# Attention and its output product of a two-layer decoder trunk: a fifth output slab is split ahead of the join, head statistics move behind a product step, and row scaling moves from VectorE to ScalarE

## The reference

```python
sc = jnp.einsum('bqhcd,bkhcd->bhcqk', qb, kb) * scale      # 8 heads, 2 components c of width 64
p = jax.nn.softmax(jnp.where(causal, sc, NEG_INF), axis=-1)
a = p[:, :, 0] - lam * p[:, :, 1]
outs.append(jnp.einsum('bhqk,bkhe->bqhe', a, vb))          # e = 128
...
o = rms_norm(o, sub_norm) * (1.0 - lam_init)
x = x + o.reshape(b, s, N_HEADS * V_DIM) @ w_o
x = x + squared_relu_mlp(rms_norm(x, mlp_norm[l]), w_up[l], w_down[l])
```

## Time and profile before

| | |
|---|---|
| median of 3 runs | 1116.8 us (1116.67 to 1117.65) |
| profiled execution | 1118.27 us, span 1116.5 us |
| PE busy in the span | 1097.5 us (98%) |
| DVE, ACT, POOL busy | 788.3, 478.8, 77.4 us |
| chain that ended last | PE 94%, DVE 3%, ACT 1% |
| attention heads 0 to 7, in the span | about 641 to 743 us |
| output product after the join and first MLP unit | from about 754 us |

### The profile page before, as it was taken

One profiled execution on the slowest core, in us unless ns is written; L12 is line 12 of the kernel. 1 busy time (PEld: TensorE's weight loads), 2 busy tenths in 40 slices (PEclk: granted clock), 3 DMA queues, 4 the chain that ended last, 5 costly groups with the idle time before them and its releaser, 6 DMA issues.

```text
span 1116.5 us, 13390 instructions
## 1 busy us (share of the span) xinstructions
PE 1097.5 (98%) x5168; PEld 904.3 (81%) x5168; DVE 788.3 (71%) x980; ACT 478.8 (43%) x695; POOL 77.4 (7%) x58
## 2 busy tenths in 40 slices
PE   8999999999999999999999998899999999999998
PEld 7888888888888888888888776677888888888887
DVE  4766554787787787688754577946668678678686
ACT  6221233453353353355532466834544344344343
POOL 0000012000000000002410211013100000000000
PEclk9999999999999999999999999999999999999999
DMA  7433462315315215201322300142323423414302
GB/s 189 104 87 108 144 203 77 114 38 172 93 39 187 76 64 163 76 1 58 113 95 76 113 1 20 58 151 86 104 75 111 116 76 117 127 59 139 87 1 76
DMA packets 144751, 105.89 MB, mean 95 GB/s; under 512 B 12592, under 2 KB 121136, under 8 KB 144688
## 3 DMA queue, kind: packets, MB, share of 16 engines
q1 hardware_dynamic: 143648, 105.03, 30.8%
q10 hardware_dynamic: 1040, 0.00, 0.1%
HBM read 102.93 MB, written 2.10 MB: 94 GB/s over the span
## 4 chain that ended last, share of the span: by engine, by line
PE 94%; DVE 3%; issue 1%; ACT 1%; DMA 1%; SPq 0%; ACTq 0%; DVEq 0%
PE ps L586 31%; PE ps L613 27%; PE ps L473 19%; PE ps L675 10%; PE ps L700 2%; PE ps L761 1%; DVE nmax L1508 1%; PE ps L739 1%; DMA kv<-in_x 1%; PE ps L751 0%; PE ps L555 0%; DVE h L1544 0%; PE ps L720 0%; PE ps L568 0%; PE ps L649 0%
## 5 line engine op out<-in xcount | busy, mean ns | idle before, releaser
L586 PE MATMUL ps<-h,w_hi 128*128 128x512 f32 x1024 | 316.2, 390 | 0.0
L613 PE MATMUL ps<-w_hi,h 128*128 128x512 f32 x896 | 277.3, 389 | 0.0
L586 PEld LDWEIGHTS ps<-h,w_hi 128*128 128x128 f32 x1024 | 191.6, 188 | 39.4
L473 PE MATMUL ps<-h,w_hi 128*128 128x512 f32 x640 | 198.6, 392 | 2.0 <-DVE h L1544 1.6
L586 PE MATMUL ps<-h,w_lo 128*128 128x512 f32 x512 | 199.3, 389 | 0.0
L613 PEld LDWEIGHTS ps<-w_hi,h 128*128 128x128 f32 x896 | 168.2, 188 | 34.8
L613 PE MATMUL ps<-w_lo,h 128*128 128x512 f32 x448 | 174.3, 389 | 0.0
L931 ACT ACTIVATE w_hi<-b_raw 128x1024 fp32r<-128x1024 f32 x80 | 82.0, 1054 | 141.4 <-PE ps L586 81.9
L473 PEld LDWEIGHTS ps<-h,w_hi 128*128 128x128 f32 x640 | 118.9, 188 | 26.8 <-DVE h L1544 1.8
L473 PE MATMUL ps<-h,w_lo 128*128 128x512 f32 x320 | 124.6, 389 | 0.0
L1245 DVE TENSOR_TENSOR w_lo<-b_raw,w_hi 128x1024 fp32r<-128x1024 f32 x80 | 95.9, 1223 | 26.7 <-ACT w_hi L931 26.7
(11 more groups left out here) (132 smaller groups left out, 1190.0 us busy)
## 6 DMA issues: line engine op xcount, KB each, us to landing
b_raw<-in_w_down SPq DMA_DIRECT2D x64, 512.0 KB, 4.5
w_raw<-in_w_up SPq DMA_DIRECT2D x64, 512.0 KB, 4.0
w_raw<-in_a_w_in SPq DMA_DIRECT2D x23, 512.0 KB, 3.7
w_raw<-in_w_kv SPq DMA_DIRECT2D x16, 512.0 KB, 3.7
w_raw<-in_a_w_out SPq DMA_DIRECT2D x8, 512.0 KB, 4.0
w_raw<-in_w_q SPq DMA_DIRECT2D x8, 512.0 KB, 3.5
w_raw<-in_w_o SPq DMA_DIRECT2D x8, 512.0 KB, 4.1
kv<-in_x SPq DMA_DIRECT2D x4, 512.0 KB, 6.9
```

Source lines behind the costliest of these rows:

```text
L473: last = nc.tensor.matmul(ps[:, bank, :], w[:, s, k * P:(k + 1) * P], src(half, k), start=(k == 0 and i == 0), stop=(k == KC - 1 and i == 2))
L586: last = nc.tensor.matmul(ps[:, v % 4, :], w[:, s_, k * P:(k + 1) * P], h_of[inp][:, half, k, :], start=(k == 0 and i == 0), stop=(k == KC ...
L613: last = nc.tensor.matmul(ps[:, CHAIN[p][tb], :], op[half][:, k, tb * P:(tb + 1) * P], w[:, s_, cols], start=(FRESH[p] and k == 0 and i == ...
```

## The change

It has five parts. (1) The fifth output slab (number 4) gets a buffer of its own, `w_fifth`, and both halves are written right after the last head's steps; PE does heads 0 to 6 of it between `out_T` of the last head and the join. `WO_SPLITS` then begins with slab 5 alone. (2) In the MLP's first quarter the copies of the first two transposed chunks are written ahead of a slab's `w_hi`. (3) `out_ms` moves behind `weights` in its step. (4) The squares are taken from the copy in SBUF instead of PSUM, after `evacuate`, and PE waits for the copy alone. (5) For heads 0 to 6 four ScalarE operations of 128x128 (`scale_o`) take the place of the one VectorE operation `out_norm`; head 7 keeps it. In `weights` the factor is made by a scalar_tensor_tensor instead of a tensor_scalar with two per-partition operands.

```diff
-WO_SPLITS = ((4, 5), (), (6,), (7,), (), (), (8,), (), (9,))
+WO_SPLITS = ((5,), (), (6,), (7,), (), (), (8,), (), (9,))
...
                 if i == 0 and h:
-                    pe.wait_ge(s_oc, 2 * h)
+                    pe.wait_ge(s_oc, 2 * h - 1)
...
             out_T(H - 1)
-            for m in range(ACC):
+            project_out(ACC, range(0, 7))
+            for m in range(ACC + 1):
                 project_out(m, range(7, 8)).then_inc(s_used, 1)
-            for m in range(ACC, KC):
-                if m > ACC:
-                    wait_acc(U_WO + m)
+            for m in range(ACC + 1, KC):
+                wait_acc(U_WO + m)
                 wait_slab(S_WO + m)
...
                     for j in range(8):
+                        if new and j == 1:
+                            copy_x(0)
+                            copy_x(1)
                         if j < 6:
                             hi(q, j + 2)
...
-                        if new and j == 1:
-                            copy_x(0)
-                        if new and j:
+                        if new and j > 1:
                             copy_x(j)
...
                 nc.scalar.activation(o_sb, ps[:, B_O, :], ACT.Copy).then_inc(s_oc, 1)
-                nc.scalar.activation(o_sq, ps[:, B_O, :], ACT.Square).then_inc(s_oc, 1)
+
+            def square_o(h):
+                act.wait_ge(s_oc, 2 * h + 1)
+                if h:
+                    act.wait_ge(s_oms, h)
+                nc.scalar.activation(o_sq, o_sb, ACT.Square).then_inc(s_oc, 1)
+
+            def scale_o(h):
+
+                act.wait_ge(s_ors, h + 1)
+                for t in range(TB):
+                    rows = o_sb[:, t * P:(t + 1) * P]
+                    last = nc.scalar.activation(rows, rows, ACT.Copy, scale=ors[:, t:t + 1])
+                last.then_inc(s_on, 1)
...
+                if i == 0 and h:
+                    square_o(h - 1)
+                if i == 2 and h:
+                    scale_o(h - 1)
...
+            split_fifth()
             copy_o(H - 1)
+            square_o(H - 1)
             out_hi(H - 1)
...
-                V.tensor_scalar(rinv[:, b, 1:2], rinv[:, b, 0:1], rsum[:, h % 2, i, 0:1], lams[:, 5:6],
-                                ALU.mult, ALU.mult).then_inc(s_sc, 1)
+                V.scalar_tensor_tensor(rinv[:, b, 1:2], rinv[:, b, 0:1], lams[:, 5:6], rsum[:, h % 2, i, 0:1],
+                                       ALU.mult, ALU.mult).then_inc(s_sc, 1)
...
+                if n + 1 < STEPS:
+                    weights(n + 1)
                 if i == 1 and h:
                     out_ms(h - 1)
-                if n + 1 < STEPS:
-                    weights(n + 1)
                 if i == 1 and h < 4:
                     q_norm_part(4 + h)
-                if i == 2 and h:
-                    out_norm(h - 1)
```

More of the change, by code:

```diff
@@ L139, in build @@
         kv = sb("kv", [P, 16, T])
+        with nc.sbuf_tensor("w_fifth", [P, 2, SLAB], F32R) as w_fifth:
+            pass
         a_raw = sb("a_raw", [P, KC, T])
@@ L468, in product @@
                 s = slot(n)
+                hi_, lo_ = (w_fifth[:, 0, :], w_fifth[:, 1, :]) if n == S_WO + 4 else (w_hi[:, s, :], w_lo[:, s, :])
                 for k in ks:
@@ L471, in product @@
                         wait_chunk(k)
-                    for i, (w, half) in enumerate(((w_hi, 0), (w_hi, 1), (w_lo, 0))):
-                        last = nc.tensor.matmul(ps[:, bank, :], w[:, s, k * P:(k + 1) * P], src(half, k),
+                    for i, (w, half) in enumerate(((hi_, 0), (hi_, 1), (lo_, 0))):
+                        last = nc.tensor.matmul(ps[:, bank, :], w[:, k * P:(k + 1) * P], src(half, k),
                                                 start=(k == 0 and i == 0), stop=(k == KC - 1 and i == 2))
@@ L1086, in copy_o @@
                     act.wait_ge(s_oT, h)
+                nc.scalar.activation(o_sb, ps[:, B_O, :], ACT.Copy).then_inc(s_oc, 1)
+            def square_o(h):
+                act.wait_ge(s_oc, 2 * h + 1)
+                if h:
                     act.wait_ge(s_oms, h)
-                nc.scalar.activation(o_sb, ps[:, B_O, :], ACT.Copy).then_inc(s_oc, 1)
-                nc.scalar.activation(o_sq, ps[:, B_O, :], ACT.Square).then_inc(s_oc, 1)
+                nc.scalar.activation(o_sq, o_sb, ACT.Square).then_inc(s_oc, 1)
[5 more added lines that the diff above has]
+                last.then_inc(s_on, 1)
             def out_hi(h):
@@ L1093, in out_hi, with split_fifth @@
                 nc.scalar.activation(h2[:, 0, h, :], ps[:, B_T, :], ACT.Copy, scale=hgs[:, 2:3]).then_inc(s_hi, 1)
+            def split_fifth():
+                n = S_WO + 4
+                act.wait_ge(s_raw[n % RAW], 16 * (raw(n) // RAW + 1))
+                nc.scalar.activation(w_fifth[:, 0, :], w_raw[:, n % RAW, :], ACT.Copy).then_inc(s_whi, 1)
             for n in range(16, 20):
@@ L1545, in out_lo, with split_fifth @@
                                        ALU.mult, ALU.subtract).then_inc(s_lo, 1)
+            def split_fifth():
+                n = S_WO + 4
+                dve.wait_ge(s_whi, n + 1)
+                V.tensor_tensor(w_fifth[:, 1, :], w_raw[:, n % RAW, :], w_fifth[:, 0, :].bitcast(F32),
+                                ALU.subtract).then_inc(s_wlo, 1)
             for n in range(16, 20):
```

## The result

The changed kernel takes 1121.8 us (median of 6 runs, 1121.24 to 1122.67), the kernel before beside it 1116.74 us (6 runs, 1116.64 to 1117.65): the ratio is 1.0042 with a 95% interval of 1.0032 to 1.0051. It is slower by 5.1 us by the medians and by 4.6 us by the fastest runs. The profiled execution took 1121.33 us, 3.06 us more than that of before.

A forecast was written before the change was run, and what follows sets the result against it. PE was taken to bound the kernel (busy 1097.5 of 1116.5 us), VectorE setting the pace in heads 5 and 6. Terms 2.1 + 0.1 + 0.8 - 0.1 + 1.7 + 0.3 - 1.2 = +3.7 on 1116.8 gave 1120.5 us, range 1117.0 to 1123.5.

The forecast's parts named there:

- heads 4 and 5: Period follows weights, statistics, GpSimd's power, scaled copies, slab's high part: 11.21 against 10.16 us, +1.05 us in each head.
- the join: Before the MLP: early fifth slab starts the residual chain 2.7 us later, against 1.0 us of slack: +1.7 us.
- head 1: Head 1 and the rest of head 2: PE's projections cover the scaling, cost 0; without cover 1.08 us a head.
- Head 6: Head without a slab: `out_T` comes 7.83 us after `out_lo` instead of 7.70, +0.1 us.
- Head 3: Split at i = 3, where PE's transposes set the pace: two cheaper factors, -0.1 us.
- End of head 2: Scaled copies' 1.08 us enters ScalarE's queue ahead of slab 0's high part, minus 0.3 slack: +0.8 us.
- The rival: Gap at the join lowers PE's clock: +1.0 us, 1121.5 to 1122 us; chance 0.22.
- MLP: Removed wait for the transposed-stream copies, -1.2 us, and the norm sums, +0.3 us.
- the norm sums: Behind MLP unit 0, they follow the same residual chain as the join: +0.3 us.
- The faster case: Scaling leaves the path if heads 4 and 5's high part ends before 718.04: 1111.5 or 1115.5 us; chance 0.14.

The follow-up runs named there:

- the swap: Changed kernel with the four scaled copies behind the slab's high part on ScalarE in heads 4 and 5 (high part first): 1119.87 us.
- `copy_x` alone: Kernel before with only the two copies of the transposed stream put ahead of a slab's high part: 1115.51 us.
- statistics and squares alone: Kernel before with fifth slab in two pieces, transposed-stream copies moved, new factor instruction, statistics behind weights, squares from copy; row scaling left on VectorE: 1113.68 us.
- the chain loosened: Changed kernel with each residual one step earlier on VectorE, ahead of the previous chunk's low part: 1120.18 us.
- statistics first: Changed kernel with the statistics ahead of the weights again on VectorE: 1122.57 us.
- fifth slab alone: Kernel before with only the early fifth slab, its own buffer and its two splits added: 1119.7 us.
- fifth slab in two: Kernel before with transposed-stream copies moved and the fifth slab split: three groups ahead of head 7 of the slabs, five behind: 1114.68 us.
- the two programs without a PE wait at the join: Ten runs: all five parts, scaled copies behind the slab, fifth slab in two, residuals earlier, 1114.41 us; five runs: the fastest kernel, 1112.07 us.
- the fastest kernel: Kernel before with fifth slab in two pieces, transposed-stream copies moved, new factor instruction and each residual one step earlier: 1112.07 us.

## Why the prediction was right

The forecast was slower, 1120.5 us; 1121.8 was measured. The two large terms, heads 4 and 5 and the join, hold in path and size, and experiments show both. One term, head 1, was wrong, and a drop of the clock that the sum left out stands in the medians. Point by point, from the two profiles:

- **Heads 4 and 5: +1.05 each forecast, +1.10 measured** (11.26 for 10.16). The path is the one I followed; the scaled copies were 0.1 dearer (1.18 for 1.08). That their place in front of the slab is the cause is shown by the swap, which gives 10.22.
- **Head 6: +0.1 forecast.** The last slices start 22.47 us after head 5's end (745.10 - 722.63), 22.26 before: +0.2 for heads 6 and 7.
- **Head 3: -0.1 forecast, +0.1 measured.** It took 13.55 us (686.56 to 700.11), for 13.46 in the heads of the kernel before without a drop (the profile of `copy_x` alone). Without the scaling (statistics and squares alone) it took 13.31: the copies cost about 0.2 us here, for which I had no term.
- **End of head 2: +0.8 forecast.** VectorE's wait for slab 0's high part ended later by about that: from head 2's last query split to `out_lo` 6.36 us for 5.54. The changed kernel, then the kernel before:

```profile
680.20 0.75 DVE L1524 SCALAR_TENSOR_TENSOR h<-ps,hgs,h 128x512 fp32r<-128x512 f32 x1 [0.86 <-ACT h L1062]
686.56 0.74 DVE L1572 SCALAR_TENSOR_TENSOR h<-ps,hgs,h 128x512 fp32r<-128x512 f32 x1
```

```profile
680.03 0.75 DVE L1496 SCALAR_TENSOR_TENSOR h<-ps,hgs,h 128x512 fp32r<-128x512 f32 x1 [0.19 <-ACT h L1058]
685.57 0.75 DVE L1544 SCALAR_TENSOR_TENSOR h<-ps,hgs,h 128x512 fp32r<-128x512 f32 x1
```

- **Heads 1 and 2 otherwise: 0 forecast, +0.5 measured. This is the step that failed**, the term in which I took PE's projections to hide all of the scaling. The sign for it, PE busy for 13.94 of 14 us, was a share over a stretch and did not say which wait would end last at `out_T`. The projections of step i = 3 stand behind `out_T` in PE's queue and can't cover it: `out_T` now waits for the copies themselves. The changed kernel, head 1:

```profile
666.16 1.27 ACT L1104 ACTIVATE work<-work,ors 128x128 f32<-128x128 f32 x4
...
667.48 0.65 PE L776 MATMUL ps<-ident,work 128*128 128x128 f32 x4 [0.22 <-ACT work L1104]
```

Before, it waited for nothing:

```profile
667.39 0.60 PE L773 MATMUL ps<-ident,work 128*128 128x128 f32 x4
```

The attention of the changed kernel's execution began 0.33 us earlier (its first scores stand at 638.82, for 639.15), so `out_T` comes 0.4 us later than before. That the copies do it shows in the run of the statistics and squares without the scaling: there head 1, from the query split before its start to `out_lo`, takes 16.84 us, for 16.80 in the kernel before and 17.66 in the changed kernel (which regains 0.36 of this in head 2).

- **The join: +1.7 forecast, +1.8 measured** (38.94 - 37.10), with residual 0 at 763.87 and a gap of 3.53 us where I had 3.5. That the residual chain sets it is shown twice: with 12 matmuls less ahead of the chain the edit gains, and with the chain loosened the gap falls to the forecast 1.90 us.
- **MLP: -0.9 forecast, -1.1 measured**, from unit 0's start to the end of the span: 335.46 for 336.56. `copy_x` alone gives 335.13, so its part is 1.4 for my 1.2, and the norm sums cost the 0.3 that I had.
- **The clock.** The rival's mechanism, a drop of the clock behind the gap at the join, does occur. I priced it at 1.0 us and gave it 0.22. It struck four of the five profiles with a gap of 1.9 us or more there; the fifth, that of the changed kernel itself, kept 1.00 through its 3.53 us. Where the gap was the same or nearly so, a drop made the way to unit 0 longer by 1.0 (statistics first), 1.9 (fifth slab alone) and 2.1 us (slab's high part first). Two of the changed kernel's six runs had a mean clock of 1.00 and took 1121.2 and 1121.3 us; the other four had 0.996 to 0.998 and took 1121.6 to 1122.7, which puts the median 0.6 us above the fastest.

The terms add up: 1.3 (heads 1 and 2) + 0.1 + 2.2 + 0.2 + 1.8 - 1.1 = +4.5 us (4.57 before rounding), and the fastest runs differ by 4.6. The two profiles differ by only 3.06, because that of the kernel before contains the drop in head 3, 1.24 us, and began its attention 0.33 us later. My +3.7 was 0.9 short of this: 0.5 in head 1, 0.2 in head 3, and 0.1 each in heads 4 and 5 together, in heads 6 and 7, and at the join, less 0.2 in the MLP. It lies nearer to the profiles' 3.06 by luck, since the drop in head 3 was no term of it.

The faster case failed where the prediction put its turning point: the high part of the slab ended at 708.88 in head 4, 8.8 us after the head's start, where 7.6 would have been in time. What is not settled is what starts a drop. At the join it came behind gaps of 1.90 to 3.53 us, and in heads 3 and 4 after waits of no more than 1.33 us; no run here was made to tell that apart.

## What to carry to other kernels

In this kernel, idle time of the bounding engine was worth removing only if the work put into it didn't push back what starts a longer chain: look for the next wait that has little slack, here 1.0 us at the end of 20 us of turn-taking between VectorE and ScalarE, and put in only as much as covers the gap. Taking an operation off a full engine gained nothing where it then stood on another queue behind a third engine and ahead of what the first one needs next. Where the order is free, write the item that waits for someone else behind the one that is ready: that gave back 1.0 us a head. It did not make the move pay: four scaled copies took 1.27 us for VectorE's 0.68, and `out_T` waited for them. A busy share of 99% is no proof that a new wait is covered: look at what stands behind the waiting item in its own queue.

## What the runs showed of the hardware that I had not expected

- The granted clock of PE fell to 0.50 in the middle of attention, in head 3 of the kernel before, and in head 4 of the fifth slab alone and of the fifth slab in two, after waits of 1.33 us and less. It stayed there for about 3.5 us in the first and 6.5 us in the last. At the join it stayed for some 3 us (residuals a step earlier, statistics first) to 6 us (fifth slab alone, high part first). In other executions of the same program it didn't fall. In head 3 the drop cost 1.24 us; head 4 took 12.11 us in the profile of the fifth slab in two, for 10.16 in that of the kernel before.
- Of the two programs without a PE wait at the join, one had ten runs within 0.6 us of each other, all with a mean clock of 1.00; the other had four runs within 0.2 us and a fifth 2.0 us above them, with a mean clock of 0.997.
- A scalar_tensor_tensor on one column took 220 ns, a tensor_scalar with two per-partition operands 273 ns, for the same product (the columns are those of `weights`' factor).
- Four ScalarE operations of 128 columns with a per-partition scale took 1.27 us, one VectorE operation on all 512 columns 0.68 us.
- Operations of VectorE and GpSimd that overlapped took longer, each time the one that started second. In the changed kernel the low part of a slab (128x1024) took 1.22 to 1.23 us on VectorE while GpSimd was idle, and 1.58 to 1.59 us each of the four times that GpSimd was already adding squares (781.52 for 1.34 us, low part at 782.36). In the fastest kernel one low part started first (764.25) and kept its 1.21 us; GpSimd's addition, begun at 764.65, took 1.96. GpSimd's power for the head's rows took 1.01 us before, and 1.46 to 1.47 us in heads 1 to 3 of the changed kernel, where the moved statistics let it begin 0.15 us after a VectorE product of 512 columns.
